# Reading the dilated layer's past tiles as two transfers of 64 rows instead of one of 128

## The chip, the cores and the metric

The program runs on one core of one Trainium2 chip. Its time is the device time of one execution in microseconds (us); the three runs of the kernel before gave 2648.06, 2652.58 and 2653.84 us, median 2652.58. The profile is one further execution; its span, from the first to the last instruction, is 2628.4 us.

## The reference

Two decoder layers with an MLP behind each, for a prompt of 512 tokens and for 8 sequences of 8 new tokens each. The change touches one part of the odd layer, the attention of the 8 sequences' new tokens over their stored past. For each sequence the past is a window of 2048 keys and values of 16 heads of 64 numbers (float32, so a row is 1024 numbers, 4 KB):

```python
k_all = concatenate([past_k, k]);  v_all = concatenate([past_v, v])   # past: (8, 2048, 16, 64)
stats = [_dilated_gather(q, k_all, v_all, q_idx, d, w // d) for w, d in ((128, 1), (512, 4), (2048, 16))]
y = _mix_branches(stats)          # softmax over the union, weighted by how many groups hold a key
```

A key that lies more than 512 positions back counts only if its distance to the query is a multiple of 16. For the 8 new queries that leaves 8 of each 16 rows of the older 1536, and all of the last 512.

## The kernel before, in words

The kernel runs through stages one after the other: loading, the even layer's FoX attention over paged keys and values, RWKV, an MLP, the dilated layer, its output projection, a second MLP, and the output. The stage that matters here is `attend_past` as `dilated` calls it.

**Tiles.** A tile is 128 rows of 1024 numbers (512 KB) with one row on each of the 128 partitions of on-chip memory. A sequence has DILT = 10 of them: tiles 0 to 5 are *older* tiles, tiles 6 to 9 *recent* ones. An older tile takes 16 groups of 16 stored rows and reads rows 0 to 7 of each group, so partition 8g + r holds row r of group g; its source is a pattern of 16 groups (64 KB apart) by 8 rows (each 4 KB, side by side). A recent tile is 128 rows side by side, so its source is a plain pattern of 128 rows. There are 80 key tiles and 80 value tiles. `dilated_keys` tells the mask which position each partition holds; the mask is a constant computed on the host (`lc_past`).

**Issue.** `load` in `load_tile` (line 2538) issues one transfer for a tile and lets it raise the tile's semaphore by 16. Keys are issued from SyncE (SP) into 4 buffers, values from GpSimd (POOL) into 8 buffers; the last values are spread over key buffers and SP too. The first 4 key tiles are issued earlier, by `first_reads`, while the prompt's attention still runs. Every load waits until its buffer has been used: a key tile for the transposes of the tile four before it (`kt_ok`), a value tile for the products of the tile eight before it (`v_used`).

**Compute.** Each half of a key tile (512 columns) is a unit: TensorE transposes it (line 1281) after waiting for the tile's semaphore, ScalarE rounds it to 16 bits (line 1363), VectorE makes the rest (line 1383), and TensorE forms the scores (lines 1292 to 1294). The softmax of a sequence needs a maximum over partitions on POOL (line 1267, `amx`), so the value products (line 1323) follow the scores of the same tile one sequence later. Each wait on a landing is for a constant, LANDED or V_LANDED per tile of that buffer (16 where the caller says nothing).

**Other transfers that the text speaks of.** The prompt `x_prompt` is loaded at line 404 to 128 partitions and `x_sample` right behind it at line 405 to partitions 0 to 63 (64 rows of 4 KB). FoX's key pages are loaded by `load_page` as two transfers of 64 rows of 4 KB each, to the even and the odd partitions of a buffer (`dst[a:P:2]`), with LANDED=32. The new tokens' rows `out_dil_v_s` and `out_dil_k_s` are stored from partitions 0 to 63 (line 1022).

Of the kernel before, what the change touches and what calls it, by code (L numbers as in the profile page):

```python
# [13 lines left out]
P = 128  # L14
# [4 lines left out]
NDEC = NSEQ * NNEW  # L19
# [29 lines left out]
def shape_constants():  # L49
# [62 lines left out]
    dist = (3 * P + i)[:, None] - far  # L112
    odd["lc_prompt"] = log_count(dist, dist >= 0)
    keys = dilated_keys()
    q = np.arange(NNEW)
    dist = (WIN + q)[None, None, :] - keys.T[:, :, None]
# [20 lines left out]

def dilated_keys():

    early = (np.arange(96)[:, None] * 16 + np.arange(8)[None, :]).reshape(6, P)  # L140
    return np.concatenate([early, 1536 + np.arange(512).reshape(4, P)])


# [18 lines left out]
def build_trunk(nc, I, O):  # L162
# [6 lines left out]
    def sem(name):  # L169
        count[0] += 1  # L170
        live.append(nc.alloc_semaphore(name=f"{name}_{count[0]}"))
        return live[-1]
# [2342 lines left out]
    def dilated():  # L2515
        with ExitStack() as outer:
            odd_consts = sb(outer, "odd_consts", [P, width(at_od)])
            R = {k: odd_consts[:, o:o + n] for k, (o, n) in at_od.items()}
# [4 lines left out]
            K_home = [flat(vT)[:, i * 1024:(i + 1) * 1024] for i in range(4)]  # L2523
            k_in = [sem(f"k_in{i}") for i in range(4)]
            oc_in = sem("oc_in")

            def load_tile(name):

                src = I[name][0].rearrange("b w h d -> b w (h d)")
                early = src.rearrange("b (g r) n -> b g r n", r=16)  # L2530

                def load(eng, n, dst, done):
                    seq, tile = divmod(n, DILT)
                    if tile < 6:
                        a = early[seq:seq + 1, tile * 16:(tile + 1) * 16, 0:8, :].rearrange("a g r n -> (a g) r n")
                    else:
                        a = src[seq:seq + 1, 1536 + (tile - 6) * P:1536 + (tile - 5) * P, :].rearrange("a w n -> (a w) n")
                    eng.dma_start(dst[:, :], a).then_inc(done, 16)
                return load
            load_k, load_v = load_tile("state_dil_k"), load_tile("state_dil_v")  # L2540

# [7 lines left out]
            with ExitStack() as sc:  # L2549
# [70 lines left out]
                def stores(sp, a_out, d_out):  # L2620
# [15 lines left out]

            attend_past(DILT, 2, 2, 4, 8, 0, 0, (QB, QH, QL), KNEW, VNEW, load_k, load_v,
                        lambda s, t0, n: R["lc_past"].rearrange("p (t q) -> p t q", t=DILT)[:, t0:t0 + n, :].unsqueeze(2).to_broadcast([P, n, 16, 8]),
                        lambda s: R["lc_new"][0:NDEC, 8 * s:8 * s + 8].unsqueeze(1).to_broadcast([NDEC, 16, 8]), K_home, k_in)


    def add_and_store():
# [42 lines left out]
    with top:  # L2685
        with ExitStack() as even:
            decay = sb(even, "decay", [P, NSEQ, 8, PAGES])
            recycling(load_and_turn)(decay)
            recycling(fox)(decay)
        recycling(rwkv)()  # L2690
        recycling(mlp)(UP0, DOWN0, 1)
        recycling(dilated)()
        recycling(project_mixed)(ODOUT, 2)
        recycling(mlp)(UP1, DOWN1, 3)
        recycling(add_and_store)()
# [34 lines left out]
```

## Time and profile before

| | |
|---|---|
| median of 3 runs | 2652.58 us (2648.06 to 2653.84) |
| span of the profiled execution | 2628.4 us |
| that execution's own time | given by the span alone; the median of the runs is 24.2 us above it |
| TensorE busy | 2264.2 us (86% of the span) |
| VectorE, ScalarE, GpSimd busy | 1440.4, 872.6, 342.1 us |
| key tiles of the dilated past | 80 transfers of 512 KB from SP, median 12.7 us from issue to landing |
| value tiles of the dilated past | 78 of 512 KB from POOL (12.8 us) and 2 from SP |

The page cuts the span into 40 slices of 65.7 us; its DMA line gives the mean busy share of the 16 DMA engines in tenths, its GB/s line what they moved. A window of the trace gives the same for any stretch. The DMA share can come out slightly above 1.00, because the durations of packets overlap a little. The landing time of a transfer includes the time in which it stands behind others.

### The profile page before, as it was taken

How to read it: one execution, taken by the hardware profiler on the slowest of the kernel's cores; microseconds unless marked ns; L12 is line 12 of the kernel's file. 1: busy time of each engine (PE TensorE's matmuls, PEld its weight loads, DVE VectorE, ACT ScalarE, POOL GpSimd, SP SyncE). 2: the span in 40 equal slices, each digit the busy share in tenths (PEclk: the TensorE clock that was granted, in tenths of full speed). 3: DMA queues.
4: the chain of work that ended last, by engine and by line, in shares of the span. 5: the costliest groups of instructions: out<-in, count | busy, mean ns of one | idle time of the engine just before them, and what ended most of it. 6: DMA issues, size and time to landing. Idle time of an engine off the chain costs nothing. (4 is left out here: it accounts for less than half of the span.)

```text
span 2628.4 us, 63413 instructions
## 1 busy us (share of the span) xinstructions
PE 2264.2 (86%) x26373; PEld 1765.9 (67%) x26373; DVE 1440.4 (55%) x2317; ACT 872.6 (33%) x1577; POOL 342.1 (13%) x434
## 2 busy tenths in 40 slices
PE   6788888888978987799999989997777776999998
PEld 3566777776737864577777757655666654777776
DVE  2436788885565546654422365476666657453223
ACT  2335444442231222333312221165333323333222
POOL 2003233331000000111100000033111110111000
PEclk8898899998978987899999989998878888999999
DMA  7323899995250034123233224444999921332331
GB/s 251 107 81 124 282 380 381 375 379 189 74 192 19 4 105 132 56 73 89 80 97 89 88 79 138 145 129 111 267 288 278 277 82 39 91 88 81 89 89 61
DMA packets 306664, 392.62 MB, mean 149 GB/s; under 512 B 23680, under 2 KB 224714, under 8 KB 306404
## 3 DMA queue, kind: packets, MB, share of 16 engines
q1 hardware_dynamic: 276580, 282.15, 35.0%
q0 software_dynamic: 29824, 106.71, 12.4%
q8 instruction: 198, 3.24, 0.5%
q14 instruction: 62, 0.51, 0.1%
HBM read 378.11 MB, written 10.70 MB: 148 GB/s over the span
## 5 line engine op out<-in xcount | busy, mean ns | idle before, releaser
L836 PE MATMUL bank<-yT,WH 128*128 128x288 f16 x3200 | 533.0, 290 | 45.9 <-DVE yT L690 34.6
L836 PEld LDWEIGHTS bank<-yT,WH 128*128 128x128 f16 x3200 | 314.2, 99 | 144.8 <-issue 48.8
L900 DVE SCALAR_TENSOR_TENSOR WL<-wring,WH 128x1024 f16<-128x1024 f32 x194 | 255.1, 1319 | 258.4 <-ACT WH L880 258.3
L1383 DVE TENSOR_TENSOR KL<-bank,KH 128x512 f16<-128x512 f32 x416 | 281.0, 687 | 174.5 <-ACT KH L1363 166.2
L1363 ACT CAST KH<-bank 128x512 f16<-128x512 f32 x416 | 242.3, 584 | 360.5 <-PE bank L1281 358.5
L836 PE MATMUL bank<-uT,WH 128*128 128x288 f16 x2048 | 338.2, 288 | 10.6 <-DVE WL L900 10.6
L836 PE MATMUL bank<-yT,WL 128*128 128x288 f16 x1600 | 331.8, 290 | 0.0
L880 ACT ACTIVATE WH<-wring 128x1024 f16<-128x1024 f32 x194 | 203.5, 1054 | 266.2 <-PE bank L836 221.4
L836 PEld LDWEIGHTS bank<-uT,WH 128*128 128x128 f16 x2048 | 201.6, 99 | 63.4 <-DVE WL L900 11.2
L836 PE MATMUL bank<-uT,WL 128*128 128x288 f16 x1024 | 210.9, 288 | 0.0
L836 PE MATMUL bank<-hT,WH 128*128 128x288 f16 x960 | 164.0, 295 | 29.1 <-DVE hT L727 18.7
L836 PEld LDWEIGHTS bank<-yT,WL 128*128 128x128 f16 x1600 | 158.4, 99 | 42.0
L1281 PE MATMUL bank<-cst,vTd 128*128 128x128 f32 x640 | 125.9, 330 | 50.1 <-DMA vTd<-in_state_dil_k 48.1
L1323 PE MATMUL bank<-vslot,ST 128*16 128x128 f32 x2720 | 111.4, 315 | 27.3 <-ACT ST L1368 25.2
L836 PEld LDWEIGHTS bank<-hT,WH 128*128 128x128 f16 x960 | 96.1, 101 | 57.0 <-DVE WL L900 30.2
L1281 PEld LDWEIGHTS bank<-cst,vTd 128*128 128x128 f32 x640 | 82.5, 165 | 61.9 <-DMA vTd<-in_state_dil_k 54.7
L1292 PE MATMUL bank<-QH,KH 128*128 128x16 f16 x1024 | 104.2, 172 | 23.0 <-DVE KL L1383 22.5
L836 PEld LDWEIGHTS bank<-uT,WL 128*128 128x128 f16 x1024 | 100.8, 98 | 26.2
L1525 POOL DMA_INDIRECT vslot<-in_cache_fox_v,vrow_of x91 | 93.9, 1032 | 148.9 <-PE bank L1323 127.0
L957 DVE TENSOR_SCALAR rd<-bank 128x288 f32<-128x288 f32 x64 | 29.2, 457 | 148.7 <-PE bank L836 148.7
L1292 PEld LDWEIGHTS bank<-QH,KH 128*128 128x128 f16 x1024 | 88.3, 98 | 32.9 <-DVE KL L1383 30.1
L954 POOL TENSOR_TENSOR uT<-qa,uT 128x288 f32 x64 | 54.5, 852 | 406.4 <-ACT uT L948 406.4
(457 smaller groups left out, 3967.9 us busy)
## 6 DMA issues: line engine op xcount, KB each, us to landing
wring<-in_ada_w SPq DMA_DIRECT2D x96, 512.0 KB, 4.6
vTd<-in_state_dil_k SPq DMA_DIRECT2D x80, 512.0 KB, 12.7
vslot<-in_state_dil_v POOLq DMA_DIRECT2D x78, 512.0 KB, 12.8
yT<-in_cache_fox_k SPq DMA_DIRECT2D x128, 256.0 KB
krows<-in_cache_fox_k SPq DMA_DIRECT2D x128, 256.0 KB
wring<-in_mlp_up SPq DMA_DIRECT2D x64, 512.0 KB, 4.1
wring<-in_mlp_down SPq DMA_DIRECT2D x64, 512.0 KB, 3.9
wring<-in_ev_w_in SPq DMA_DIRECT2D x26, 512.0 KB, 3.8
```

Of the source, the lines that this page charges most:

```text
L836: last = nc.tensor.matmul(bank[b + h][:, 0:HALF], w[s % 2][:, c, :], x[:, s % parts * KC + c, h * HALF:(h + 1) * HALF], start=(s % parts = ...
L880: nc.scalar.mul(WH[s % 2][:, :, :], w[:, :, :], WSCALE).then_inc(high_ok, 1)
L900: nc.vector.scalar_tensor_tensor(WL[s % 2][:, :, :], w[:, :, :], WSCALE, WH[s % 2][:, :, :], ALU.mult, ALU.subtract).then_inc(w_free, 1)
L954: nc.gpsimd.tensor_tensor(chunk_at(rest, oc, 0, HALF), qa[:, :], chunk_at(high, oc, 0, HALF), ALU.subtract).then_inc(rest_a, 1)
L957: nc.vector.tensor_scalar(rd[:, :], ps[:, 0:HALF], 0.0, 0.5 / WSCALE, ALU.max, ALU.mult).then_inc(relu_d, 1)
L1281: last = nc.tensor.transpose(b[:, j * P:(j + 1) * P], K[t % KR][:, 512 * part + j * P:512 * part + (j + 1) * P], ident)
L1292: nc.tensor.matmul(o, KH[i][:, jc], QH[:, v, j, :], start=True, stop=False)
L1323: last = nc.tensor.matmul(o[32 * j:32 * j + 16, 256 * e:256 * e + P], st[:, u, 16 * j:16 * j + 16], rows[:, 512 * part + j * P:512 * part ...
L1363: nc.scalar.copy(KH[i][:, :], turned[n % NT][:, :]).then_inc(hi_out, 1)
L1383: nc.vector.tensor_tensor(KL[i][:, :], turned[n % NT][:, :], KH[i][:, :], ALU.subtract).then_inc(lo_out, 1)
L1525: nc.gpsimd.indirect_dma_start(dst[:, :], None, v_rows, bass.IndirectOffsetOnAxis(ap=vrow_of[:, n:n + 1], axis=0), bounds_check=320 * PAGE ...
```

## The change

An older tile is now read by two transfers of 64 rows: rows 0 to 3 of all 16 groups go to partitions 0 to 63, rows 4 to 7 to partitions 64 to 127. A recent tile is also read in two, its first 64 rows and its last 64. Both raise the same semaphore, so every wait is for 32 per tile. The mask's list of positions is permuted to match. Buffers, order of issue, and all compute stay the same.

```diff
 def dilated_keys():
-    early = (np.arange(96)[:, None] * 16 + np.arange(8)[None, :]).reshape(6, P)
+    early = (np.arange(96)[:, None] * 16 + np.arange(8)[None, :]).reshape(6, 16, 2, 4).transpose(0, 2, 1, 3).reshape(6, P)
     return np.concatenate([early, 1536 + np.arange(512).reshape(4, P)])
...
                 def load(eng, n, dst, done):
                     seq, tile = divmod(n, DILT)
-                    if tile < 6:
-                        a = early[seq:seq + 1, tile * 16:(tile + 1) * 16, 0:8, :].rearrange("a g r n -> (a g) r n")
-                    else:
-                        a = src[seq:seq + 1, 1536 + (tile - 6) * P:1536 + (tile - 5) * P, :].rearrange("a w n -> (a w) n")
-                    eng.dma_start(dst[:, :], a).then_inc(done, 16)
+                    for half in range(2):
+                        if tile < 6:
+                            a = early[seq:seq + 1, tile * 16:(tile + 1) * 16, 4 * half:4 * half + 4, :].rearrange("a g r n -> (a g) r n")
+                        else:
+                            first = 1536 + (tile - 6) * P + 64 * half
+                            a = src[seq:seq + 1, first:first + 64, :].rearrange("a w n -> (a w) n")
+                        eng.dma_start(dst[64 * half:64 * half + 64, :], a).then_inc(done, 16)
...
-                        lambda s: ..., K_home, k_in)
+                        lambda s: ..., K_home, k_in, LANDED=32, V_LANDED=32)
```

## Rows read from the trace of the kernel before

**Rows 1.** The page: busy times, and its DMA and GB/s lines in 40 slices.

```profile
PE 2264.2 (86%) x26373; PEld 1765.9 (67%) x26373; DVE 1440.4 (55%) x2317; ACT 872.6 (33%) x1577; POOL 342.1 (13%) x434
DMA  7323899995250034123233224444999921332331
GB/s 251 107 81 124 282 380 381 375 379 189 74 192 19 4 105 132 56 73 89 80 97 89 88 79 138 145 129 111 267 288 278 277 82 39 91 88 81 89 89 61
```

**Rows 2.** Windows: us, five engines' busy time, PEclk, DMA share, GB/s; the stage.

```profile
1811.00:2113.00 302.00, 225.72 (x4078) 198.92 (x4079) 191.12 (x334) 105.74 (x184) 46.16 (x86) 0.79 1.00 273
...
1843.00:1860.00 17.00, 14.04 (x243) 12.73 (x242) 10.77 (x20) 7.27 (x13) 2.39 (x4) 0.80 0.78 216
1860.00:2107.00 247.00, 190.19 (x3528) 166.83 (x3525) 159.26 (x280) 86.48 (x150) 38.82 (x73) 0.81 1.02 282
```

**Rows 3.** Who waited for whom, 1810 to 2115 us: total, times, longest.

```profile
POOL vslot L2538 <- PE bank L1323: 178.3, 35, 9.5
...
POOL amx L1267 <- DVE cmx L1412: 74.2, 8, 36.0
...
PE bank L1281 <- DMA vTd<-in_state_dil_k: 48.1, 35, 4.0
...
PE bank L1323 <- ACT ST L1368: 25.2, 8, 3.7
```

**Rows 4.** Transfers of the dilated past by tensor: issue ns min/median/max, times.

```profile
L2538 SPq DMA_DIRECT2D vTd<-in_state_dil_k x80: 327/536/2160, 1727.2 to 2087.8; - x80
...
L2538 POOL DMA_DIRECT2D vslot<-in_state_dil_v x78: 515/530/737, 1810.9 to 2109.1; - x78
```

**Rows 5.** Key transfers issued from 1884 to 1896 us, then from 1900 to 1917 us.

```profile
L2538 SPq DMA_DIRECT2D vTd<-in_state_dil_k x3: 333/334/536, 1884.4 to 1894.5; - x3
...
L2538 SPq DMA_DIRECT2D vTd<-in_state_dil_k x4: 536/540/548, 1902.5 to 1913.8; - x4
```

**Rows 6.** SyncE's timeline before the stage: start, us, engine, line, transfer, count.

```profile
1719.80 0.39 SPq L1022 DMA_DIRECT2D out_dil_v_p<-vrowsd  x1
1720.24 0.52 SPq L1022 DMA_DIRECT2D out_dil_v_s<-VNEWd  x1
```

**Rows 7.** Windows: recent keys and recent values in flight together (2 of 4 places).

```profile
1896.00:1899.00 3.00, 3.00 (x68) 2.80 (x70) 1.94 (x5) 1.99 (x4) 1.05 (x2) 1.00 1.02 408
...
2044.00:2047.00 3.00, 3.00 (x71) 2.63 (x60) 2.62 (x5) 1.37 (x3) 1.05 (x2) 1.00 1.01 385
```

**Rows 8.** Windows: older tiles in flight, deep queues.

```profile
1735.00:1741.00 6.00, 4.65 (x20) 2.70 (x22) 2.95 (x10) 5.38 (x18) 2.36 (x4) 0.72 1.03 261
...
1873.00:1893.00 20.00, 14.90 (x243) 13.23 (x244) 10.90 (x23) 5.95 (x11) 2.74 (x5) 0.69 1.03 264
...
1908.70:1923.30 14.60, 11.02 (x192) 9.99 (x191) 8.50 (x18) 4.41 (x8) 1.33 (x3) 0.77 1.03 291
...
1946.50:1960.50 14.00, 10.56 (x216) 9.74 (x208) 8.88 (x19) 4.68 (x8) 2.59 (x5) 0.87 1.03 280
2021.00:2035.00 14.00, 10.94 (x212) 10.22 (x208) 7.54 (x16) 4.68 (x8) 1.59 (x3) 0.88 1.03 282
2058.00:2073.00 15.00, 10.32 (x207) 9.46 (x205) 9.92 (x20) 5.16 (x9) 2.45 (x5) 0.84 1.03 272
```

**Rows 9.** Windows: older tiles just after the queues had started afresh or were short.

```profile
1816.00:1822.00 6.00, 2.00 (x32) 1.79 (x28) 1.94 (x4) 1.03 (x2) 0.00 (x0) 0.75 1.02 226
1838.50:1842.00 3.50, 1.92 (x30) 1.70 (x28) 1.89 (x4) 1.17 (x2) 0.00 (x0) 0.50 1.02 214
```

**Rows 10.** Windows: x_prompt alone, then x_sample alone, both at the kernel's start.

```profile
6.00:10.00 4.00, 0.45 (x5) 0.35 (x4) 0.23 (x1) 0.00 (x0) 0.41 (x1) 1.00 1.02 417
11.20:11.90 0.70, 0.00 (x0) 0.00 (x0) 0.00 (x0) 0.00 (x0) 0.70 (x1) 1.00 0.87 176
```

**Rows 11.** A window in the FoX stage.

```profile
300.00:500.00 200.00, 167.44 (x3506) 148.20 (x3507) 160.54 (x260) 92.07 (x159) 75.04 (x76) 0.96 0.99 375
```

**Rows 12.** FoX's key transfers, 64 rows to the even or odd partitions: issue ns.

```profile
L1515 SPq DMA_DIRECT2D yT<-in_cache_fox_k x128: 482/483/880, 194.5 to 584.6; - x128
```

More of the change, by code:

```diff
@@ L2638, in dilated @@
                         lambda s, t0, n: R["lc_past"].rearrange("p (t q) -> p t q", t=DILT)[:, t0:t0 + n, :].unsqueeze(2).to_broadcast([P, n, 16, 8]),
-                        lambda s: R["lc_new"][0:NDEC, 8 * s:8 * s + 8].unsqueeze(1).to_broadcast([NDEC, 16, 8]), K_home, k_in)
+                        lambda s: R["lc_new"][0:NDEC, 8 * s:8 * s + 8].unsqueeze(1).to_broadcast([NDEC, 16, 8]), K_home, k_in, LANDED=32, V_LANDED=32)
     def add_and_store():
```

## The prediction

> **What bounds the kernel now.** I read the page's slices first. TensorE is busy most of the time nearly everywhere, so over the whole span it looks like the bound; but in slices 29 to 32 the DMA line shows four nines while the GB/s line shows only 267 to 288 [rows 1]. Slices 6 to 9, in FoX, have the same nines at 375 to 381 GB/s. So the dilated past is a stretch in which the DMA engines never rest and yet move a quarter less than they can. That is the stretch that the change touches.
>
> Next come windows of this stage. From 1811 to 2113 us it is 302 us long and moves 273 GB/s; in its main part, 247 us, the DMA share is 1.02 and the rate 282 GB/s, with TensorE busy 190 of 247 us; only 17 us near its start show a share of 0.78 [rows 2]. The waits say how the rate reaches the end: TensorE waits 48.1 us for landings of key tiles, and 25.2 us for the exponents; POOL waits 178.3 us for TensorE to free value buffers [rows 3]. So the value loads are led by TensorE, TensorE by the key landings, and these by the shared DMA engines. All of it is a loop through a saturated resource: a lower DMA rate lengthens the stage one for one, a higher one shortens it until TensorE is the bound.
>
> The third reading is why the rate is 282 and not 400. The stage has two kinds of tile. Where recent keys and recent values are in flight together, the rate is 385 to 408 GB/s [rows 7]; older tiles run at 261 to 291 with deep queues (the first of these rows is the four first key tiles, alone) [rows 8] and at 214 to 226 where transfers had just started together or few were queued [rows 9]. Which tiles are in flight in such a window I took from the issue times and the 12.7 us to landing; in most of rows 8 both streams are on older tiles, with an edge of the other kind. The remaining bytes move in mixed stretches near the stage's mean.
>
> Two further rows bear on what a 64-row transfer does. x_prompt goes to 128 partitions at 417 GB/s; x_sample, 64 rows side by side in HBM to partitions 0 to 63, follows at 176 GB/s, with a DMA share of 0.87, which is 202 GB/s per full share [rows 10]. Source addresses can't explain that (256 KB in one piece); what differs is that only half of the partitions are written. FoX's 64-row key transfers go to every second partition and their stage runs at 375 GB/s [rows 11, 12]; so it is not the number of rows but their lying in one half of the partitions. Half of the partitions takes about half of the rate: 202 of 417.
>
> The Trainium skill ("SBUF — State Buffer", section "Door 1: The DMA port swizzle") says the same of partitions 0 to 63: they reach 8 of 16 ports. That goes against this change, and so does the page's next rule, which is weighed as a rival below.
>
> **Why older tiles are slow now.** Issue times split into two classes: 333 ns for recent tiles, 536 to 548 ns for older ones [rows 5]. A plain 128-partition store issues in 0.39 us, a 64-partition one in 0.52 [rows 6]. So the transfer with a source of 16 groups by 8 rows is cut among the 16 engines in another way than a plain one of 128 rows. My reading, an inference, is that each engine gets one group of 8 neighbouring partitions and walks over them, and that engines then meet on the same part of the memory's width, while plain 128-row transfers keep them apart. The rates fit: engines in step 214 to 226, about the half-width level of 202; engines out of step 261 to 291.
>
> **The change part by part.** (1) Every tile, older or recent, becomes a first transfer that writes only partitions 0 to 63, and then a second for 64 to 127. An engine now has 4 rows in the lower half, then 4 in the upper, and so on. If two engines are at the same point they share a half of the width; if they are 4 rows apart they don't. That is the same alternation that I infer for the older tiles now, so I price it by their rows. What is lost for certain is the clean pattern of the recent tiles (64 of 160 transfers), whose joint stretches run at 385 to 408.
>
> (2) The sum. After 1811 us the stage loads 76 key and 80 value tiles, 156 x 0.524288 MB = 81.8 MB. At the 282 GB/s of the main part that is 290 us; the other 12 us of the 302 are start, the 17 us stretch at 0.78 and the end [rows 2]. I keep those 12 and put T = 81.8 MB / r + 12. The rows for r: 261, 264, 291, 280, 282, 272 deep (mean 275), 226 and 214 in step. T is then 310 at 275, 317 at 268, 322 at 264, 325 at 261, 374 at 226, 394 at 214; at 291 it is 293. The whole stage is now of this kind, without the recent tiles' clean stretches that let engines drift apart between one run of older tiles and the next, so I go below the mean of the deep rows, by part of the way to the rows in step: r = 268. T = 305 + 12 = 317, which is 15 us more than 302.
>
> (3) More transfers. SP issues 160 instead of 80, at 0.52 to 0.57 us each, 1.1 us per tile; a key tile's turn is 302/76 = 4.0 us, and SP has no other work there, so it is hidden. POOL issues about 78 more at 0.54 us, 42 us in all, beside 178 us in which it waits for TensorE [rows 3, 4]. What stands behind them on POOL is the next load and, 8 times, the maximum over partitions (`amx`), for which VectorE's subtraction, the exponent and the value products wait: at most 8 x 0.54 = 4.3 us if it were late each time; POOL waited 74.2 us for its input in those 8 cases, so I take 0. If the cover went (POOL busy), the value loads would come 0.54 us later each, still inside an 8-tile queue.
>
> (4) Twice the completion signals (16 small packets for each transfer). FoX, with 256 KB key transfers, has a share of 0.99 at 375 GB/s [rows 11], so they cost little; bounds 0 and 3 us (1% of the stage), taken as 0. Waiting for 32 instead of 16 adds no wait: the two halves are issued about 0.5 us apart and use the same engines. A gain from the first half's early landing is excluded, since nobody uses a half tile. The permuted mask costs nothing: same shape, same instructions.
>
> The sum is +15 us on the profiled execution, whose span is 2628.4 us; the median of the runs lies 24.2 us above that span, and I carry the difference over unchanged: 2652.6 + 15 = 2668 us.
>
> **The rivals.**
>
> *A, the forecast:* recent tiles lose their clean pattern, older ones keep theirs; r between 255 and 274. T from 311 to 333, +9 to +31. For it: rows 8 and the alike issue classes. Against it: the spread of these rows is as large as the effect.
>
> *B, engines stay in step.* All engines are on the lower half together, then on the upper, and nothing in the stage drives them apart any more. Place: the two DMA queues through the stage; price: r 214 to 235, T = 394 to 360, +58 to +92. It decides if the start's 226 [rows 9] continues past 1825 us. For it: x_sample's 202 and the start. Against it: older key tiles alone held 261 GB/s for 6 us without falling back into step [rows 8]. The Trainium skill ("SBUF — State Buffer", "Can I just issue two DMAs to hit both halves?") says that two transfers, at partition 0 and partition 64, gained only 6% over one, because they serialize. As an estimate from its figures, 218 GB/s for 64 partitions with 6% more is 231 GB/s, so T = 366 us and +64. No row here shows two such transfers together.
>
> *C, faster, the other side.* Two forms. With 4 neighbouring partitions per engine, engines fixed in their place of the width could pair up 4 rows apart, one on each half; then all tiles run as rows 7. At 395 GB/s the DMAs would need 207 + 12 = 219 us, less than TensorE's 226 us of busy time in the stage, so T would be about 235 to 255 us: -47 to -67. The point from which it decides is a rate over 300 GB/s for older tiles. Weaker: r at the best deep row, 291, gives T = 293, -9 us. For it: half of the stage's packets are slow today and this regroups them, and the 16-by-8 source pattern, if it is the culprit by its addresses, is now 16 by 4. Against it: nothing orders the two engines so.
>
> *D, nothing changes.* Losses on recent tiles and gains in the mixed stretches cancel: r between 277 and 288, T 296 to 307. For it: the deep rows' mean of 275 is near the main part's 282.
>
> **How the numbers follow.** This kernel's measurement can tell about 0.2%, 5.3 us, from no change. A 0.45, B 0.20, C 0.17, D 0.18. A and B are slower (0.65), D is within 0.2% (0.18), C is faster (0.17). The predicted time is A's, 2668 us. The range must reach D and C's weak form on one side and much of B on the other: 2643 (r 291) to 2725 (r 226, +72). Left out are the strong form of C (about 0.08) and the end of B (about 0.1). A's own range is 2661 to 2684.
>
> **What would show it.** Right, if windows of the stage show no stretch above 320 GB/s any more, a DMA share still at 1.02, older and recent tiles at one rate near 268, and TensorE's waits for key landings up from 48 to about 60 us; all key transfers then issue in the 0.5 us class. B shows as 215 to 235 throughout. C shows as a rate above 300 with TensorE's waits near FoX's, and a wrong reading of the half width. If the time changes outside 1811 to 2113 us, or key landings are late while the DMA share is below 0.95, the prediction is wrong in its ground and not only in its size.

## The result: slower by 1.4%, all of it in the dilated past, at 247 GB/s

The changed kernel takes 2684.79 us (median of 4 runs, 2683.89 to 2687.21) against 2650.32 for the one before (4 runs, 2640.35 to 2653.84). The ratio of the two is 1.0143, 95% interval 1.0112 to 1.0175, so it lost 38 us (30 to 46). The forecast was 2668, +15: the measured time is inside its range (2643 to 2725), and sign and place came out as forecast, but the loss was forecast too small by more than half.

The page of the changed kernel, the same lines as [rows 1] (here the slices are 67.1 us wide):

```profile
PE 2288.5 (85%) x26373; PEld 1783.2 (66%) x26373; DVE 1438.7 (54%) x2317; ACT 869.8 (32%) x1577; POOL 380.5 (14%) x512
DMA  7423899996250034123233234527999941332331
GB/s 242 109 84 130 305 344 357 365 354 207 73 188 18 4 120 119 48 85 88 79 91 91 77 104 139 164 67 167 242 252 245 249 108 48 86 87 80 91 91 59
```

The four slices of the dilated past still show nines, now at 242 to 252 GB/s instead of 267 to 288. Windows of the changed kernel (us; five engines' busy time; PEclk, DMA share, GB/s) give the stage, its main part, a piece of its start, three stretches and FoX:

```profile
1827.00:2169.00 342.00, 243.89 (x4099) 213.16 (x4101) 193.71 (x335) 105.80 (x184) 84.05 (x164) 0.73 1.02 241
1885.00:2160.00 275.00, 200.65 (x3394) 174.23 (x3393) 153.53 (x266) 84.06 (x146) 67.02 (x132) 0.73 1.03 247
1836.00:1856.00 20.00, 9.75 (x125) 8.94 (x123) 7.16 (x11) 4.69 (x8) 0.00 (x0) 0.50 1.03 219
1885.00:1915.00 30.00, 22.71 (x352) 19.73 (x351) 15.04 (x29) 8.25 (x15) 6.47 (x13) 0.58 1.04 220
1925.00:1955.00 30.00, 20.41 (x368) 18.25 (x368) 18.42 (x34) 8.83 (x15) 6.66 (x13) 0.82 1.03 271
1995.00:2045.00 50.00, 36.94 (x618) 31.69 (x619) 29.23 (x51) 16.49 (x29) 13.27 (x27) 0.74 1.03 244
300.00:500.00 200.00, 163.88 (x3333) 143.19 (x3322) 151.06 (x248) 85.40 (x150) 71.67 (x72) 0.93 0.97 358
```

The stage went from 302 to 342 us, the main part from 282 to 247 GB/s at a share of 1.03 [rows 2]. The stretches of 385 to 408 GB/s [rows 7] are gone: cut into pieces of 3 us, the main part has none above 288. The rate wanders: 219 to 220 in stretches of 20 and 30 us, 271 for 30 us, about 244 for most of the rest.

The waits of the stage and the transfers, against [rows 3, 4]:

```profile
POOL vslot L2540 <- PE bank L1323: 174.5, 34, 10.0
PE bank L1281 <- DMA vTd<-in_state_dil_k: 75.6, 42, 4.9
POOL amx L1267 <- DVE cmx L1412: 70.2, 8, 35.7
```

```profile
L2540 SPq DMA_DIRECT2D vTd<-in_state_dil_k x160: 465/594/2358, 1743.4 to 2140.3; - x160
...
L2540 POOL DMA_DIRECT2D vslot<-in_state_dil_v x156: 498/526/726, 1827.1 to 2164.4; - x156
```

TensorE's wait for key landings rose by 27.5 us (48.1 to 75.6). Its busy time rose too, from 226 to 244 us for the same matmuls, at a granted clock of 0.73 instead of 0.79: in the starved stretch from 1836 to 1856 us the clock is 0.50, its lower level (1.2 GHz), with TensorE busy 9.75 of 20 us. So a part of the lateness is hidden in longer matmuls; the reader who looks at the waits alone finds only 27.5 of the 40 us. I read the longer matmuls as a consequence and no cause, because the DMA share is 1.03 to 1.04 in the stretches with a low clock too (1836 and 1885 us); no run tests this by itself.

The two profiled spans differ by 54 us, 2682.4 against 2628.4, not by 38. The stage has 40 of it, and it starts 16 us later (1827 against 1811), while what follows it is 2 us shorter. Nearly all of the 16 lies in FoX, which runs at 358 GB/s here and at 375 before [rows 11] with the same instructions. The second profile of the kernel before, below, tells whose they are.

### The profile page after: what moved, and what is told of

The parts are those of the page before. It is cut to its first block and busy times, and to the rows that moved or that the text cites. A ratio compares the mean times of both kernels' runs of the same rounds, so it can differ in the third digit from the quotient of the medians.

```text
span 2682.4 us, 63573 instructions
## 1 busy us (share of the span) xinstructions
PE 2288.5 (85%) x26373; PEld 1783.2 (66%) x26373; DVE 1438.7 (54%) x2317; ACT 869.8 (32%) x1577; POOL 380.5 (14%) x512
## 5 line engine op out<-in xcount | busy, mean ns | idle before, releaser
L1281 PE MATMUL bank<-cst,vTd 128*128 128x128 f32 x640 | 136.0, 350 | 77.8 <-DMA vTd<-in_state_dil_k 75.6
L1281 PEld LDWEIGHTS bank<-cst,vTd 128*128 128x128 f32 x640 | 88.9, 175 | 91.5 <-DMA vTd<-in_state_dil_k 84.9
L1323 PE MATMUL bank<-vslot,ST 128*16 128x128 f32 x2720 | 120.0, 333 | 23.7 <-ACT ST L1368 21.5
```

The costliest lines, as they stand in the source:

```text
L1281: last = nc.tensor.transpose(b[:, j * P:(j + 1) * P], K[t % KR][:, 512 * part + j * P:512 * part + (j + 1) * P], ident)
L1323: last = nc.tensor.matmul(o[32 * j:32 * j + 16, 256 * e:256 * e + P], st[:, u, 16 * j:16 * j + 16], rows[:, 512 * part + j * P:512 * part ...
```

## The experiments

Times of the stage run from the first value issue to the last landed data, from one profile each. Ratios compare whole kernels with runs of the kernel before on the same chip. e5, e6, e7 and e12 read other rows than the layer needs, as many as before, so only their times are of use. The diffs are cut to the transfers (that of e9 to e11 also has the list of positions); the mask and the counts waited for follow them. Main parts run from 50 us after the stage's start to 6 before its end; cut so (1877 to 2163 us), the changed kernel's has 246 GB/s. Four theories are tested. W: a transfer to one half of the partitions is slow by itself. N: the number of transfers costs. S: older tiles are slow by their source distance. P: older tiles are slow by the shape of their pattern, 16 by 8, and how it is cut among the engines.

### Even and odd partitions (e1)

```diff
-    eng.dma_start(dst[64 * half:64 * half + 64, :], a).then_inc(done, 16)
+    eng.dma_start(dst[half:P:2, :], a).then_inc(done, 16)
```

> Every tile is still read as two transfers of 64 rows, but the first goes to the even partitions and the second to the odd ones, as FoX's key pages do. Theory W (a transfer to one half of the partitions is slow, and the change made all of them so): the rate in the stage rises above 340 GB/s, the stage of 341 us falls to 240 to 270 us, the whole kernel to 2585 to 2620 us, below both kernels. Theory N (twice as many transfers of half the size are what costs): nothing changes against the changed kernel, 341 us and 2685 us. Theory S (older tiles are slow because of their source addresses 64 KB apart): recent tiles recover (385 GB/s where both streams are recent), older ones stay at 250 to 280 GB/s, stage 295 to 310 us.

Measured: 0.9962 (0.9939 to 0.9986), stage 293 us. So N falls: the same number of transfers of the same source rows, in the same order, and the stage is 49 us shorter than the changed kernel's 342. Only the partitions that each transfer writes differ between the two. But W's number was missed too, 293 and not 240 to 270. Recent tiles recovered (three 3 us pieces of the main part are at 388 to 402 GB/s), older ones did not, which was S's forecast, but for a stage 2 us below its 295.

### Which tiles carry the loss (e2, e3)

```diff
 # e2: older tiles in halves, recent ones whole     # e3: the reverse
-    eng.dma_start(dst[:, :], a).then_inc(done, 16)
+    eng.dma_start(dst[:, :], a).then_inc(done, 32)   # the kind that stays whole
```

> Only older tiles are split into lower and upper half; a recent tile is one transfer to 128 partitions as before (it raises its semaphore by 32, so the wait for 32 holds for both kinds). Theory W with the reading of the prediction (older tiles already had this alternation): the stage is 302 to 312 us, stretches near 400 GB/s are still there, the kernel within 10 us of the one before. Rival H (two halves in separate transfers keep the engines in step more than one walk over 8 partitions did): stage 320 to 335 us, older stretches 215 to 250 GB/s.

> Only recent tiles are split into two halves of the partitions; older tiles are one transfer as before (raising by 32). Theory W: the stretches near 400 GB/s vanish, the rest stays at 255 to 285 GB/s, stage 310 to 325 us, kernel 10 to 20 us slower than before. Rival H (the split of older tiles carries the loss): stage below 308 us.

Measured: e2 0.9982 (0.9956 to 1.0008), stage 290 us; e3 1.0160 (1.0124 to 1.0197), stage 346 us. Halving the older tiles costs nothing, and the stage is even below the 302 to 312 us expected; halving the recent ones alone costs as much as the whole change, the kernel 42 us by the ratio against the 10 to 20 us expected. Windows of the main part, e1, e2, e3 in this order:

```profile
1872.00:2109.00 237.00, 184.10 (x3477) 162.23 (x3475) 157.40 (x278) 85.22 (x147) 69.72 (x136) 0.81 1.03 288
```

```profile
1871.00:2105.00 234.00, 184.04 (x3478) 163.90 (x3476) 156.88 (x276) 84.80 (x147) 56.77 (x111) 0.81 1.02 293
```

```profile
1868.00:2158.00 290.00, 209.08 (x3570) 182.52 (x3566) 161.98 (x281) 87.62 (x151) 51.12 (x98) 0.72 1.03 242
```

All three are saturated. In e3 only 64 of 160 tiles are halved, yet the whole main part is at 242 GB/s, older stretches included: its 3 us pieces go from 201 to 288, most of them near 240.

### The kernel before again (e4)

> The kernel before, unchanged, for a second profile. In the profile of before, FoX's main stretch ran at 373 to 383 GB/s, and in the profile of the changed kernel at 347 to 366, though neither kernel differs there. If that is a matter of the execution or the chip, this profile shows FoX between 347 and 383 GB/s and a span of 2628 to 2655 us, with the dilated stage at 302 us within 5 us. If the dilated stage itself varies by more than 5 us, the 39 us between the two profiles is not all due to the change.

Measured: 0.9990 (0.9968 to 1.0011), stage 301 us, and its FoX window:

```profile
300.00:500.00 200.00, 167.67 (x3354) 145.34 (x3354) 151.38 (x249) 86.46 (x153) 72.07 (x72) 0.92 0.97 358
...
1875.00:2119.00 244.00, 186.54 (x3464) 164.22 (x3463) 156.47 (x274) 85.38 (x148) 37.86 (x71) 0.80 1.02 281
```

The stage repeats within 1 us; FoX does not, 358 against 375 GB/s in the same program. The time ahead of the stage is therefore not the change's. Over all profiles FoX's window gave 352 to 364 GB/s in e1 to e8, which ran on one chip, and 374 to 382 in e9 to e15, which ran on two others, whatever the kernel. Whether the chip itself, the placement of data or something else makes the difference was not separated.

### Source and shape (e5, e6, e12), and halves with a dense source (e7)

```diff
-    a = early[seq:seq + 1, tile * 16:(tile + 1) * 16, 0:8, :]     # groups 64 KB apart
+    a = dense[seq:seq + 1, tile * 16:(tile + 1) * 16, :, :]       # e5: side by side
+    a = src[seq:seq + 1, tile:WIN:16, :]                          # e6: 128 single rows, 64 KB apart
+    a = near[:, :, 0:8, :]                                        # e12: groups 36 KB apart
```

> The kernel before, but an older tile reads 16 groups of 8 rows that lie side by side (128 neighbouring rows, the wrong ones, so that attention works on other keys); pattern shape, destination and issue class stay. Theory S (older tiles are slow because their groups lie 64 KB apart in HBM): the stage's rate rises to 370 to 400 GB/s where nothing else binds, the stage falls from 301 us to 225 to 250 us. Theory P (the 16-by-8 pattern is cut among the engines in a way that makes them meet on the same partitions): nothing changes, 281 GB/s, 300 us.

> The kernel before, but an older tile reads one row of each of 128 groups 64 KB apart as a plain pattern of 128 rows (the wrong rows). Theory S: slow, 240 to 290 GB/s in the older stretches, stage 285 to 340 us, and each issue in the 0.33 us class. Theory P: all tiles are plain now, so 370 to 400 GB/s and a stage of 225 to 250 us.

> The kernel before, but an older tile reads 16 groups of 8 rows whose groups lie 36 KB apart instead of 64 KB (the wrong rows); the pattern can't be merged into a plain one, as it could in the dense case. Theory P: as before, 275 to 285 GB/s, stage 295 to 305 us, issues in the 0.54 us class. Theory S: stage 240 to 260 us.

> The changed kernel, but its older tiles read neighbouring groups (the wrong rows), so that all sources are dense and only the half-of-the-partitions destinations are left. Theory W (the lower and upper half as separate transfers cost width by themselves): 230 to 260 GB/s, stage 325 to 360 us, as in the changed kernel's 342. If the loss needs the far source addresses as well: above 300 GB/s, stage under 285 us.

Measured: e5 0.9751 (0.9709 to 0.9794), stage 240 us; e6 0.9762 (0.9721 to 0.9803), 241 us; e12 1.0011 (0.9985 to 1.0037), 301 us; e7 1.0129 (1.0084 to 1.0175), 342 us. The key transfers of e5, e6 and e12, then the main parts of e6 and e12:

```profile
L2539 SPq DMA_DIRECT2D vTd<-in_state_dil_k x80: 327/328/2386, 1748.8 to 2051.7; - x80
```

```profile
L2538 SPq DMA_DIRECT2D vTd<-in_state_dil_k x80: 327/328/2350, 1750.0 to 2053.5; - x80
...
1882.00:2067.00 185.00, 157.21 (x3304) 139.99 (x3304) 146.44 (x262) 80.89 (x140) 35.67 (x67) 0.90 0.94 351
```

```profile
L2539 SPq DMA_DIRECT2D vTd<-in_state_dil_k x80: 327/536/2124, 1730.9 to 2089.8; - x80
...
1865.00:2110.00 245.00, 185.46 (x3485) 163.35 (x3481) 158.76 (x280) 85.34 (x148) 37.74 (x71) 0.82 1.02 281
```

S falls: at 64 KB distance a plain pattern runs at 351 GB/s (its share is 0.94, so here the loads no longer saturate the engines all the time; 370 to 400 was expected), and at 36 KB the 16-by-8 pattern runs at the old 281. e5 alone would have misled: groups side by side merge into a plain pattern, as the median issue of 328 ns shows, so it changed the shape as well. Among whole tiles the issue class told the two kinds apart, as [rows 5] had hinted. e7 says that halves cost the same 342 us without any far source. How the engines are assigned to partitions in either kind is not visible in the trace and stays an inference.

### Order of the halves (e8)

```diff
-    for half in range(2):
+    for half in ((0, 1) if name == "state_dil_k" else (1, 0)):
```

> The changed kernel, but values issue the upper half first and keys the lower half first. Theory W with engines in step: an engine that alternates between the two queues now alternates between the halves, so fewer meet on one half; 265 to 300 GB/s, stage 285 to 320 us, kernel 20 to 50 us faster than the changed one. Without a role of being in step: no change, 342 us within 5 us.

Measured: 1.0196 (1.0158 to 1.0234), stage 353 us, 237 GB/s. Not 20 to 50 us faster but slower than the changed kernel, and outside the 342 us within 5 of the other forecast too. My picture of engines that fall in step and can be set apart by order is not supported.

### The change on plain patterns alone (e9, e10, e11)

```diff
+    far = np.arange(8)[:, None] + np.arange(P)[None, :] * 16        # tile r: row r of all 128 groups
+    rest = (1536 + 8 + np.arange(32)[:, None] * 16 + np.arange(8)[None, :]).reshape(2, P)
...
+    if tile < 8:
+        a = src[seq:seq + 1, tile:WIN:16, :]                        # e9: whole, 128 partitions
+        first = tile + 1024 * half; a = src[seq:seq + 1, first:first + 1009:16, :]   # e10: to dst[64 * half:64 * half + 64]
+        first = tile + 16 * half; a = src[seq:seq + 1, first:first + 2017:32, :]     # e11: to dst[half:P:2]
```

> The same 1280 keys per sequence in other tiles: eight tiles hold row r (0 to 7) of all 128 groups, a plain pattern of 128 rows 64 KB apart; two tiles hold rows 8 to 15 of the last 32 groups in the 16-by-8 pattern. All are single transfers to 128 partitions. Theory P (the 16-by-8 pattern, not the distance, makes a transfer slow): 330 to 390 GB/s in the eight plain tiles, stage 240 to 265 us against 301 before, kernel 2590 to 2615 us. Theory S (source distance): stage 300 us or more.

> As e9, but each of the eight plain tiles is read as two transfers of 64 rows, to partitions 0 to 63 and 64 to 127 (the two other tiles stay whole). The change of the study on plain patterns alone. Theory W (a half-of-the-partitions destination costs by itself): 235 to 260 GB/s and a stage of 325 to 350 us. If halves cost only together with the group pattern: stage under 290 us.

> As e9, but each of the eight plain tiles is read as two transfers of 64 rows, to the even and to the odd partitions. Theory W: as e9, within 15 us in the stage. Theory N (number of transfers): as e10.

Measured, against the kernel before: e9 0.9895 (0.9866 to 0.9924), e10 1.0120 (1.0080 to 1.0161), e11 0.9876 (0.9841 to 0.9912). Their stages are 274, 346 and 272 us; e9's lies above the 240 to 265 expected, e10's and e11's as W has them:

```profile
1817.00:2091.00 274.00, 214.00 (x4060) 190.15 (x4063) 189.22 (x333) 106.05 (x184) 46.51 (x86) 0.82 0.93 300
```

```profile
1811.00:2157.00 346.00, 239.03 (x4104) 210.89 (x4107) 193.93 (x335) 106.13 (x184) 77.80 (x150) 0.73 1.01 238
```

```profile
1803.00:2075.00 272.00, 210.20 (x4068) 186.83 (x4069) 189.37 (x333) 105.58 (x184) 79.27 (x150) 0.85 0.93 303
```

This is the study's change on plain patterns, with the same keys on the same partitions, and two transfers instead of one for 8 of 10 tiles. To even and odd partitions it costs nothing, to lower and upper ones 72 us of stage and 64 us of the kernel (medians). The source rows of one transfer lie 128 KB apart in e11 and 64 KB in e10; between e1 and the changed kernel even these are the same, and the difference is there too. So what costs is which partitions a transfer writes, and N is excluded. That a transfer to one half is slow alone, with nothing beside it, rests on x_sample only [rows 10].

Windows of e9 say why its stage is longer than expected: plain tiles, then the 16-by-8 ones, then the border between two sequences:

```profile
2047.00:2056.00 9.00, 6.33 (x158) 6.08 (x156) 7.20 (x17) 2.95 (x6) 1.65 (x3) 1.00 1.03 406
2005.00:2008.00 3.00, 2.32 (x54) 1.65 (x50) 2.96 (x6) 1.06 (x2) 0.32 (x1) 1.00 1.02 238
2056.00:2062.00 6.00, 5.24 (x84) 4.26 (x84) 2.88 (x6) 2.66 (x6) 1.05 (x2) 0.72 0.65 193
```

Plain rows 64 KB apart reach 406 GB/s, as fast as the recent tiles of [rows 7], where 330 to 390 was expected. The two tiles left in 16-by-8 form pull the rate down to about 240, and at each border the engines are no longer saturated, so something else binds there; what it is was not looked into.

### Does one stream slow the other, and are all halves alike (e14, e15)

```diff
 # e14: the changed kernel, recent tiles too as 16 groups by 4 rows
+    a = src[...].rearrange("a (g r) n -> a g r n", r=8)[:, :, 4 * half:4 * half + 4, :]
 # e15: e9 with halves for keys alone
+    if tile < 8 and name == "state_dil_k":  # two transfers, as e10
```

> The changed kernel, but the recent tiles are halved as the older ones are: rows 0 to 3 of 16 groups of 8 rows to the lower partitions, rows 4 to 7 to the upper (the mask permuted to match). All transfers now go to halves, all with a 16-by-4 source pattern. If what keeps e2 fast is its whole recent tiles: as the changed kernel, 240 to 255 GB/s, stage 335 to 350 us. If plain 64-row halves are worse than 16-by-4 halves: above 265 GB/s, stage below 320 us.

> As e9, but the eight plain tiles are halved for keys alone; values are whole transfers to 128 partitions. If a stream in halves slows the other stream too (both share engines and the width): both streams near 240 to 265 GB/s together, stage 310 to 345 us, values' packets as slow as the keys'. If each stream pays only for itself: halfway between e9 and e10 or better, stage 280 to 310 us.

Measured: e14 1.0086 (1.0052 to 1.0119), stage 330 us; e15 1.0082 (1.0055 to 1.0110), stage 323 us. Main parts:

```profile
1852.00:2126.00 274.00, 200.38 (x3549) 175.90 (x3538) 159.73 (x278) 86.74 (x151) 70.23 (x140) 0.76 1.03 255
```

```profile
1861.00:2128.00 267.00, 197.99 (x3481) 173.56 (x3478) 157.95 (x275) 85.30 (x148) 37.99 (x71) 0.75 1.02 260
```

e15 lies nearer to e10 than to e9: with only the keys halved, the saturated rate is 260 GB/s, though every value transfer is whole. If each stream paid for itself, equal bytes at e10's 244 and e9's 308 would give 272 (an estimate). The packets say it more clearly: in e15's stage the mean 4 KB packet takes 254 ns on the values' queue and 258 on the keys', where e9 has 204 and 198 and e10, with both in halves, 275 and 273. So a stream in halves slows the other. e14's rate of 255 GB/s is at the edge of what it was to show if pattern made no difference, and its stage of 330 us is below it (335 to 350): group halves are a little better than plain ones (one profile each). But with no whole transfer left the stage is still 40 us longer than e2's, whose older tiles are read in exactly the same way.

### All patterns plain (e13)

```diff
+    for j in range(4):                                  # the two tiles that e9 left in 16-by-8 form
+        first = 1536 + 8 + 4 * (tile - 8) + j
+        a = src[seq:seq + 1, first:first + 497:16, :]   # 32 rows
+        eng.dma_start(dst[j:P:4, :], a).then_inc(done, 16)
```

> As e9, but its two remaining tiles are each read as four plain transfers of 32 rows, to every fourth partition, so that no transfer has the 16-by-8 pattern (whole tiles raise by 64 to match). Theory P: the last slow stretches of e9 (packets of 245 to 270 ns) go to about 165 ns; stage 235 to 255 us against 274 in e9; kernel 15 to 35 us below e9. If transfers of 32 rows are slow whatever their partitions, or their issue (4 x 0.5 us) binds: stage 270 us or more.

Measured: 2586.02 us, ratio 0.9836 (0.9810 to 0.9861); the fastest of the kernels that compute the layer, 43 us below the kernel before by the ratio, and 18 below e9 (medians on two chips). The stage is 255 us, at the edge of what was expected. In its main part the share is 0.90, and no 3 us piece with a share of 1.00 or more is below 352 GB/s. TensorE's wait for key landings is down to 13.1 us, less than its wait for the exponents:

```profile
1855.00:2054.00 199.00, 163.23 (x3299) 145.02 (x3299) 146.36 (x261) 80.69 (x140) 53.67 (x103) 0.87 0.90 328
...
PE bank L1324 <- ACT ST L1369: 27.3, 8, 3.7
PE bank L1282 <- DMA vTd<-in_state_dil_k: 13.1, 13, 1.8
```

## Why the prediction was right, and where it was wrong

*The place and the bound: right.* The loss is in the stage, at a DMA share of 1.03, and reaches the end: 40 us in the stage, 38 in the kernel. The sum's form holds: with the measured 247 GB/s, 81.8 MB / 0.247 + 12 gives 343 us, measured 342. The 12 is a remainder of the old profile and was carried over; that it fits again was not tested apart.

*The half width: right in kind.* x_sample's 202 GB/s against x_prompt's 417 [rows 10] was read so that it matters which partitions are written; e1 against the changed kernel, and e11 against e10, show that. They do not show "about half of the rate": with lower and upper halves both queued, e10 has 244 GB/s against e11's 310. The rule of the Trainium skill ("SBUF — State Buffer", "Can I just issue two DMAs to hit both halves?"), that two transfers to the two halves gain only 6%, gave an estimate of 231 GB/s; the trace has 247, and 244 on plain patterns (e10). It was nearer than my 268, though both halves queued gain more than 6% here: some 20% over x_sample's 202, which is itself from a window of 0.7 us.

*The step that failed* is the rate in part (2) of the sum, "r = 268", and behind it the sentence of part (1) that the new alternation of halves "is the same alternation that I infer for the older tiles now, so I price it by their rows". Measured r is 247; this term alone is the difference between +15 and +41 by the formula. Two things were wrong in it. First, the older tiles' rows [rows 8] were read in a stage where whole plain transfers came between the runs of older tiles. Take these away, and the same older transfers run slower. A stretch of e2 between recent tiles, then the fastest and the slowest of six 30 us stretches of e14, whose older tiles are read alike:

```profile
1943.00:1973.00 30.00, 22.46 (x431) 19.88 (x429) 19.04 (x35) 10.84 (x19) 7.01 (x15) 0.83 1.03 284
```

```profile
1900.00:1930.00 30.00, 22.74 (x400) 19.62 (x400) 17.45 (x34) 9.83 (x18) 6.70 (x14) 0.77 1.04 268
1930.00:1960.00 30.00, 20.59 (x366) 18.31 (x363) 15.21 (x25) 8.19 (x14) 6.97 (x14) 0.77 1.04 234
```

Three more stretches of e2 give 277 to 283. The prediction had seen this danger and allowed 7 GB/s for it (275 to 268); it was worth 28 (275 to 247). And halves pull whole transfers down (e15; e3's 242 GB/s with 40% of the tiles halved, older stretches included). A rate from a mixed stage may not be carried to an unmixed one. Second, older tiles were slow by their 16-by-8 shape (e12 against e6) and not by alternating halves as such. So likeness of rate was no likeness of cause. What the shape and the halves do inside the engines stays open. That I went below the mean "by part of the way to the rows in step" was the right direction, and e2 against e14 bears out that older tiles gain from clean ones between them. The reason given, engines in step, has e8 against it and is not shown.

*Rival B* had the price of the starting stretch, 219 to 220 GB/s, and the kernel does run there from 1836 to 1856 and from 1885 to 1915 us; but it leaves this rate again without help. The outcome lies between A and B. *D* and *C* are out; C's strong form asked for 235 to 255 us of stage; e5 and e6 reached that by plain patterns (240 and 241).

*Parts (3) and (4): right.* 80 more SP issues (0.59 us each at the median, not 0.52 to 0.57), 78 more from POOL and twice the completion signals are hidden: e1 has all of them and is no slower than the kernel before, and e11, with 64 more for keys, is as fast as e9. The forecast for TensorE's waits was 60 us; they are 75.6, in line with the larger loss.

## What to carry to other kernels

Where the DMA engines are saturated, judge a transfer by which partitions it covers and by its pattern: 64 rows to every second partition were free, 64 rows to one half of the partitions cost 72 us in a stage of 274. Look at the issue time of a whole tile whose neighbours run faster: here 0.54 against 0.33 us marked the slow 16-by-8 pattern. It is no mark of slowness among smaller transfers: e11's even and odd halves issue in 0.60 us and are fast. Choosing other tiles for the same keys, so that each transfer is a plain row pattern, won 1.6%. Do not price a uniform new state by rates read in a mixed one.

## What the runs showed that I had not expected

- With older tiles as 16 groups by 8 rows to 128 partitions the main part runs at 281 GB/s whether the groups lie 64 or 36 KB apart; with 128 rows 64 KB apart in a plain pattern it reaches 351 at a share of 0.94, and 406 where the engines are saturated (e9).
- Transfers to one half of the partitions slow whole transfers of the other queue: 260 GB/s with halves on one queue alone, 308 with none, and the whole transfers' packets take 254 ns instead of 204.
- Issuing the halves in opposite order on the two queues made it worse, 237 against 247 GB/s. Why is open.
- Halving older tiles alone gave 290 us of stage against 301 (one profile each; the whole kernel 0.9982, 0.9956 to 1.0008, not told from no change).
- FoX's rate, in code that no experiment touches, was 352 to 364 GB/s in the profiles e1 to e8 (one chip) and 374 to 382 in e9 to e15 (two others).
